# A hybrid decoder step in float32: norm factors made with tokens on partitions, and other work moved between engines in the convolution mixer

## The reference, cut to what matters

```python
def rms_norm(x, g):
    return x * rsqrt(mean(x * x, axis=-1) + 1e-6) * g

def conv_mixers(h, ...):                       # h: RMS-normed input, D = 1024
    z = h @ w_in                               # 1024 -> 2560 = 20 columns of 128
    glu = z[..., :512] * sigmoid(z[..., 512:1024])
    af = causal_dwconv31(glu) + bias
    an = (af - mean(af)) * rsqrt(var(af) + 1e-5) * lg + lb   # over 512 channels
    a_out = an * sigmoid(an)
    G, C, X = z[..., 1024:1536], z[..., 1536:2048], z[..., 2048:2560]
    b_out = G * causal_dwconv3(C * X)
    return concat(a_out, b_out) @ w_out        # residual add follows
```

## Time and profile before

| | |
|---|---|
| median of 3 runs | 2745.41 us (2745.17 to 2745.77) |
| the profiled execution | 2743.18 us |
| its span | 2741.4 us |
| mean granted clock of TensorE | 0.987 |
| busy: PE, PEld | 2634.0, 2465.1 us |
| busy: DVE, ACT, POOL | 1435.6, 627.5, 782.2 us |

### The profile page before, as it was taken

One profiled execution on the slowest core, in us unless ns is written; L12 is line 12 of the kernel. 1 busy time (PEld: TensorE's weight loads), 2 busy tenths in 40 slices (PEclk: granted clock), 3 DMA queues, 4 the chain that ended last, 5 costly groups with the idle time before them and its releaser, 6 DMA issues.

```text
span 2741.4 us, 41727 instructions
## 1 busy us (share of the span) xinstructions
PE 2634.0 (96%) x17498; PEld 2465.1 (90%) x17498; DVE 1435.6 (52%) x1985; ACT 627.5 (23%) x930; POOL 782.2 (29%) x432
## 2 busy tenths in 40 slices
PE   6999699999999999999999999979999999999996
PEld 6988699999999999997777777759999999999995
DVE  6899856444444444456555555561544444444445
ACT  4110133111111111133333333342311111111111
POOL 5323325332233333340011011023433333233332
PEclk9999899999999999999999999999999999999997
DMA  6433294444444444643443444423111111111111
GB/s 198 161 131 123 92 180 167 164 168 169 169 169 169 169 168 164 219 159 123 143 167 127 166 153 155 148 91 135 47 47 47 42 44 47 47 47 47 47 42 64
DMA packets 93863, 336.70 MB, mean 123 GB/s; under 512 B 22528, under 2 KB 39808, under 8 KB 91136
## 3 DMA queue, kind: packets, MB, share of 16 engines
q1 hardware_dynamic: 93696, 334.20, 36.6%
HBM read 315.88 MB, written 152.25 MB: 171 GB/s over the span
## 4 chain that ended last, share of the span: by engine, by line
PE 87%; DVE 9%; issue 1%; ACT 1%; POOL 1%; DMA 0%; POOLq 0%; DVEq 0%; SPq 0%; ACTq 0%
PE reg L620 44%; PE reg L656 19%; PE reg L847 9%; DVE g L1458 4%; PE reg L725 3%; PE reg L827 3%; PE ob L883 2%; PE reg L868 1%; PE reg L800 1%; DVE neg_s L1685 1%; PE ob L868 1%; PE reg L936 1%; PE reg L638 1%; PE reg L923 1%; PE ob L699 1%
## 5 line engine op out<-in xcount | busy, mean ns | idle before, releaser
L620 PE MATMUL reg<-xs,w_sp 128*128 128x352 f32 x8208 | 1347.1, 326 | 33.8 <-DVE xs L1424 20.8
L620 PEld LDWEIGHTS reg<-xs,w_sp 128*128 128x128 f32 x8208 | 1335.3, 189 | 41.7 <-issue 30.3
L382 POOL TENSOR_TENSOR w_sp<-w_raw,w_sp 128x1024 fp32r<-128x1024 f32 x172 | 426.5, 2480 | 1068.2 <-ACT w_sp L377 1066.5
L656 PE MATMUL reg<-hid,w_sp 128*128 128x352 f32 x3168 | 514.3, 324 | 0.0
L656 PEld LDWEIGHTS reg<-hid,w_sp 128*128 128x128 f32 x3168 | 511.5, 188 | 0.0
L377 ACT ACTIVATE w_sp<-w_raw 128x1024 fp32r<-128x1024 f32 x172 | 182.3, 1060 | 1138.4 <-PE reg L620 713.1
L1435 DVE TENSOR_TENSOR h<-reg,h 128x1056 f32<-128x1056 f32 x200 | 251.4, 1257 | 305.0 <-PE reg L656 235.0
L847 PE MATMUL reg<-xs,w_sp 128*128 128x352 f32 x1512 | 279.6, 332 | 0.0
L1591 DVE TENSOR_TENSOR g<-reg,rst 128x1056 f32<-128x1056 f32 x44 | 55.4, 1259 | 414.7 <-PE reg L620 414.7
L847 PEld LDWEIGHTS reg<-xs,w_sp 128*128 128x128 f32 x1512 | 240.6, 189 | 17.7 <-issue 17.6
L400 POOL TENSOR_TENSOR w_sp<-w_raw,w_sp 128x1024 fp32r<-128x1024 f32 x21 | 49.9, 2375 | 479.9 <-ACT w_sp L395 461.1
(11 more groups left out here) (178 smaller groups left out, 1978.5 us busy)
## 6 DMA issues: line engine op xcount, KB each, us to landing
w_raw<-in_wstream SPq DMA_DIRECT2D x193, 512.0 KB, 3.6
out_sk<-in_cache_k SPq DMA_DIRECT2D x16, 4088.0 KB, 15.4
out_sv<-in_cache_v SPq DMA_DIRECT2D x16, 4088.0 KB, 15.3
kvr<-in_kva SPq DMA_DIRECT2D x16, 2048.0 KB, 9.3
kvr<-in_kvb SPq DMA_DIRECT2D x16, 1536.0 KB, 6.9
wt<-in_wtab SPq DMA_DIRECT2D x16, 512.0 KB, 5.1
h<-in_xT SPq DMA_DIRECT2D x4, 1056.0 KB, 10.0
h_spill<-h SPq DMA_DIRECT2D x8, 528.0 KB, 2.6
```

What stands on the lines that cost most here:

```text
L382: nc.gpsimd.tensor_tensor(w_sp[:, u % 3, 1, :], w_raw[:, u % 3, :], w_sp[:, u % 3, 0, :].bitcast(F32), ALU.subtract).then_inc(w_lo, 1)
L620: mm = nc.tensor.matmul(out[:, t, :], w[:, wh, k * P:(k + 1) * P], xs[:, xh, k, t * TS:(t + 1) * TS], start=(n == 0 and wh + xh == 0), sto ...
L656: mm = nc.tensor.matmul(out[:, t, :], w[:, wh, kk * 512 + m * P:kk * 512 + (m + 1) * P], hid[:, par_g, kk, xh, t * TS:(t + 1) * TS], start ...
```

## The change

1. **Norm factors with tokens on partitions**, at three places (first norm, LayerNorm variance, last norm). `token_sums`: nine matmuls, each with 128 tokens of `acc` as the stationary operand and one column of the 1/1024 matrix, so that the sums lie on 128 partitions x 9 columns. Square root (`compact_std`) and reciprocal (`compact_recip`) work on these 9 columns (`cs`). Nine further matmuls (`spread_sample`, `spread_half`) multiply a column of `cs`, repeated 128 times, by the identity, which puts the factors back on every partition. ScalarE copies them out of PSUM; the LayerNorm's products read PSUM directly. The norms in front of layer 0's FFN, attention and layer 1's FFN stay as they were.
2. **First squares**: eight buffers instead of two, and the sums on VectorE (`first_square`), between its `gain_lo` steps. The very last add of the last norm is on VectorE too. `rst` squared (`rst2`) is made once on ScalarE and used at C, so that POOL's product there goes.
3. **Weight remainders of units 4 to 22** are made on VectorE (`mixer_lo`), between its taps.
4. **Taps**: 96 beside the units 1 to 16; the other ten behind the input units, beside the B projection. `MEAN_USE` moves from the first to the fifth B use, `VAR_USE` from the fifth to the seventh. The sample convolution works in two halves, since `prod` gets its own, smaller place.
5. **SP**: no cache copies before unit 45; then one at every fifth unit to 90 (10 pieces), and 22 pieces at every third unit from 122 on. The states are stored one by one between unit loads 31 to 40; the waits in front of the FFN state come after unit 28.

The core of the diff (places that only follow from these are left out):

```diff
-MEAN_USE, VAR_USE = B_USE[0], B_USE[4]
+MEAN_USE, VAR_USE = B_USE[4], B_USE[6]
...
+            for u in range(3, 29):
+                load_unit(sp, u, u % 3)
             sp.wait_ge(x_lo, 2 * KD)
             sp.wait_ge(x_hi, 2 * KD)
             load_ffn_state(0)
+            for u in range(29, 95):
+                load_unit(sp, u, u % 3)
+                if 31 <= u < 41:
+                    if u == 31:
+                        sp.wait_ge(ysum_ok, 1)
+                    dst, src = states[u - 31]
+                    sp.dma_start(dst, src).then_inc(st_out, 16)
+                elif u >= 45 and u % 5 == 0:
+                    copy_piece(*pieces.pop())
...
+            for u in range(121, NUNITS + 1):
+                load_unit(sp, u, u % 3)
+                if u % 3 == 2 and pieces:
+                    copy_piece(*pieces.pop())
...
+            def token_sums(src):
+                for j, lo in enumerate(BLOCKS):
+                    mm = nc.tensor.matmul(ob[:, 1, j:j + 1], src[:, lo:lo + P], ones[:, 0:1], start=True, stop=True)
+                return mm
+            def spread_half(x):
+                for j in range(4):
+                    mm = nc.tensor.matmul(ob[:, x, j * P:(j + 1) * P], cs[:, 4 * x + j:4 * x + j + 1].to_broadcast([P, P]),
+                                          ident[:, :], start=True, stop=True)
+                return mm
...
-            first_units(0, 2, 0, 0)
+            in_proj(0, FIRST[0], x_at=0)
+            pe.wait_ge(sum_ok, KD)
+            token_sums(acc).then_inc(tk_full, 1)
+            in_proj(1, FIRST[1], part=(0,))
+            pe.wait_ge(r_ok, 1)
+            spread_sample(ob[:, 0, 0:NS]).then_inc(st_full, 1)
+            spread_half(1).then_inc(half_full, 1)
+            pe.wait_ge(std_ok, 1)
+            spread_half(0).then_inc(st_full, 1)
+            in_proj(1, FIRST[1], part=range(1, KD))
...
-                        sample_sums()
+                        token_sums(acc).then_inc(tk_full, 1)
...
+                        if k == 0 and r == VAR_USE:
+                            pe.wait_ge(r_ok, 2)
+                            spread_sample(ob[:, 0, 0:NS]).then_inc(ln_full, 1)
+                            spread_half(1)
+                            pe.wait_ge(std_ok, 3)
+                            spread_half(0).then_inc(ln_full, 1)
...
-            column_means(NAMED["stats4"], (sum_ok, SQ0[4] + KD), acc)
+            pe.wait_ge(sum_ok, SQ0[4] + KD)
+            token_sums(acc).then_inc(tk_full, 1)
+            pe.wait_ge(r_ok, 3)
+            spread_sample(reg[1][:, 0, 0:NS])
+            spread_half(1).then_inc(half_full, 1)
+            spread_half(0).then_inc(st_full, 1)
...
-                square(0, m, h[:, m, :])
+                nc.scalar.activation(sq_first[m], h[:, m, :], ACT.Square).then_inc(sq_ok, 1)
...
-            std_parts(2)
+            act.wait_ge(std_ok, 2)
+            nc.scalar.activation(rst2[:, :], rst[:, :], ACT.Square).then_inc(r2_ok, 1)
...
-            for m in range(KD):
-                add_square(0, m)
...
-                elif kind == "C":
-                    pool.wait_ge(free, FIRST[u] + 1)
-                    nc.gpsimd.tensor_tensor(tmp[:, :], tmp[:, :], rst[:, :], ALU.mult).then_inc(cr_ok, 1)
...
+            def mixer_lo(u):
+                dve.wait_ge(w_hi, cnt(u))
+                nc.vector.tensor_tensor(w_sp[:, u % 3, 1, :], w_raw[:, u % 3, :], w_sp[:, u % 3, 0, :].bitcast(F32),
+                                        ALU.subtract).then_inc(w_lo, 1)
...
             for u, (kind, c) in enumerate(MIX_ORDER):
                 mixer_step(kind, c, FIRST[u])
-                if u >= 1:
-                    for tc, tk in TAPS[PER * (u - 1):PER * u]:
+                if 1 <= u < 17:
+                    for n, (tc, tk) in enumerate(TAPS[PER * (u - 1):PER * u]):
+                        if n == 2:
+                            mixer_lo(u + 3)
                         conv_tap(tc, tk)
+                elif u in (17, 18):
+                    mixer_lo(u + 3)
             for c in range(CA):
                 rest_lo(1, c, c, cb[:, c, :])
+            mixer_lo(22)
+            rest = TAPS[PER * 16:]
+            for n, (tc, tk) in enumerate(rest):
+                if n == 3:
+                    add_to_h(B_USE[0], 0)
+                if n == 7:
+                    add_to_h(B_USE[1], 1)
+                conv_tap(tc, tk)
+            add_to_h(B_USE[2], 2)
+            add_to_h(B_USE[3], 3)
...
-            for m in range(4):
-                add_to_h(B_USE[m], m)
...
+            add_to_h(B_USE[4], 4)
+            add_to_h(B_USE[5], 5)
+            compact_recip(2)
...
             for c in range(CA):
-                nc.vector.tensor_tensor(Y[c], Y[c], tmp[:, :], ALU.mult).then_inc(yn_ok, 1)
-            add_to_h(B_USE[5], 5)
+                y = Y[c][:, 0:NP_].rearrange("p (x t) -> p x t", x=2)
+                nc.vector.tensor_tensor(y, ob[:, :, :], y, ALU.mult).then_inc(yn_ok, 1)
+                nc.vector.tensor_tensor(Y[c][:, NP_:], Y[c][:, NP_:], tmp[:, NP_:], ALU.mult).then_inc(yn_ok, 1)
```

More of the change, by code:

```diff
@@ L63, in plan_uses @@
 def plan_uses():
-    first, last, named, n = {}, {}, {}, 0
+    first, last, n = {}, {}, 0
     def unit(u, k=1):
@@ L429, in build @@
         sqb = [sil[:, PAD:], tmp[:, :]]
+        sq_first = [cb[:, 0, :], cb[:, 1, :], cb[:, 2, :], cb[:, 3, :], spare[:, :], tmp[:, :], sil[:, PAD:], g1[:, PAD:]]
+        BLOCKS = [P * j for j in range(NP_ // P)] + [T - P]
+        NBLK = len(BLOCKS)
         block = ctx.enter_context(nc.Block())
@@ L1799, in _ @@
             ffn(1)
-            factor(NAMED["stats4"], rst[:, :], 10)
+            dve.wait_ge(sq_ok, SQ0[4] + KD)
+            dve.wait_ge(sum_ok, SQ0[4] + KD - 1)
+            nc.vector.tensor_tensor(acc[:, :], acc[:, :], sqb[(SQ0[4] + KD - 1) % 2], ALU.add).then_inc(sum_ok, 1)
+            compact_recip(3)
+            dve.wait_ge(std_ok, 11)
             for m in range(KD):
```

173 lines of the change are left out of this document (81 added, 92 removed).

## The result

| | before | after |
|---|---|---|
| median, same chip | 2745.29 us (4 runs) | 2721.14 us (2719.57 to 2722.13, 4 runs) |
| profiled execution | 2743.18 us | 2722.13 us |
| its span | 2741.4 us | 2720.3 us |
| granted clock of TensorE | 0.987 | 0.989 |

The ratio of the times is 0.9911, with a 95% interval of 0.9894 to 0.9929: 0.9% faster, clear of noise, by 24 us in the medians and 21.1 us in the two traced executions. The forecast was 2722 and 23.4 us off the traced execution.

The account below looks back on a forecast made before the run. TensorE, busy 2634.0 of 2741.4 us, was taken as the bound. Gains of 1.8 + 13.1 + 5.5 + 3.0 = 23.4 us off 2743.18 gave 2719.8, and 2722 from the median; range 2711 to 2734.

Parts of the forecast that it names:

- the input units: Mixer's input units: TensorE's stops go because VectorE keeps up; gain 13.1 us, bounds 7 to 13.1.
- The ten taps: Mixer: ten taps go behind the input units, taking 13 us of VectorE's work out of them.
- Start: First norm to the end of unit 1: ends at 51.3 instead of 53.1; gain 1.8 us, bounds 6.5 to -1.5.
- Output units: End of the input units to the first A matmul: 60.6 us instead of 69.1; gain 5.5 after clock, bounds 8.5 and 0.
- the 3.0 us for the clock: Output units: taken off the 8.5 us gain because both stops can lower the clock for the matmuls behind them.
- The rival "clock": Low clock at the start, variance and end costs 2.2 + 4.4 + 1 us more: 2729; chance 0.17.
- Between the FFN and the last matmul: FFN, attention and second FFN, to the last matmul: no change, 0 us.
- End: Last matmul to first output step: that step at 2725.1 instead of 2727.81; gain 3.0 us, 2.7 to 7.1.
- Copies: Cache copies, none in the mixer and 22 of 32 beside the last FFN: priced at nothing.
- VectorE as the bound: Rival 1, the 16 units with taps and remainders: VectorE becomes the bound, 2785 us, slower; chance 0.05.
- The late chain: Rival 3, output units: the LayerNorm chain in four uses of cover is later, 8 us more, 2730; chance 0.14.
- The end at the good bounds: Rival 4, everything at its good bound: start 6.5, no clock loss, end 7, about 2710 us; chance 0.12.

Follow-up runs that it names:

- the first experiment: Changed kernel with the weight remainders of units 4 to 22 back on GpSimd: 2733.36 us, ratio to before 0.9957.
- the experiment: Changed kernel with the old norm factors at the first norm alone, first squares staying on VectorE: 2716.97 us, ratio to before 0.9899.
- the last experiments: Changed kernel with old first-norm factors, a GpSimd split held back, LayerNorm chain off GpSimd and idle matmuls: 2704.74 us; without the first of these: 2710.99 us.
- the kernel with all four edits: Changed kernel with old first-norm factors, GpSimd's third split held back, LayerNorm chain off GpSimd, 22 idle matmuls before the last token sums: 2704.74 us.
- the one without the first-norm edit: Changed kernel with GpSimd's third split held back, LayerNorm chain off GpSimd and 22 idle matmuls, token factors kept at the first norm: 2710.99 us.

## Why the prediction was right, and where it was not

**Right as a whole**: 2721.1 against 2722, by a sum in which two terms came out high and two low. That the total fits to 1 us is partly luck: between the traced executions, for which the sum was made, the gain is 21.1 us and not 23.4, and errors of 0.6 to 2.4 us per stretch cancel in part. The largest term, the input units, was right in size (13.8 for 13.1) and in its main mechanism: GpSimd's remainders made the stops in these units, and undone they bring back 11.3 us of the stretch. The ten taps, 13 us in the forecast's sum for these units, were not needed there: put back, they leave the units at 240.5 us and cost 9.5 us in front of the output units. The last 2.5 us of the 13.8 are not traced to one part; the product at C that left GpSimd and VectorE's earlier start were not tried alone. The 104 taps cost 102.5 + 40.8 = 143 us, near the 147 that the forecast left them for 105. Each remainder frees 2.1 us of VectorE by the first experiment, 37.5 us for 18 of them, where the forecast took 36 us (three quarters of the taps' excess of 48) for the remainders and the product at C together. The units took 240.5 us where I had 241.5; by the forecast's own prices (18 x 11.8 and 3 x 9.9) it should have been 242.1, and the gain 12.5.

The Trainium skill's rule that the two engines exclude each other for a whole instruction ("SBUF — State Buffer", "Who interferes with whom") would have given 2.4 per remainder; the 2.1 measured is near it.

**Start, 1.8, measured 1.2.** The sums began at 34.5, as forecast (35.0). The small matmuls at full clock are 0.12 us as I took them (2.17 / 18 = 0.12). But the clock fell behind them (0.50 from 37.3 to 40.7), which cost the spreads and the 9 matmuls between them 1.7 us. And the step priced the moved squares and the new factors in one sum and never set the new factors against the old ones: 4.5 us of small matmuls against 2.3 of column sums. With the 1.7 us of the clock that is 3.9, and the experiment shows a loss of 3.7 us on TensorE's path, inside a gain of some 5 us made by moving the squares. One edit hid the other's price.

**Output units, 5.5, measured 3.1.** The schedule held within 2 us: stops of 3.63 and 3.76 us (3.4 and 3.8), the second on GpSimd's `w_sp` (the token sums begin at E+46.0, E being the end of the input units, forecast E+44.3; the mean sums stood at E+28.5, 1.5 later than forecast, behind the first stop's clock). The term that failed is the 3.0 us for the clock. The low stretch is 10.2 us long, and from the first sum to the matmul behind the spreads it is 9.75 us (348.44 - 338.69) where the full clock gives 5.41 (337.93 - 332.52, last fence above): 4.3 us, and 1.5 more behind the first stop (25.07 for 23.6). So 5.8 us stand where the forecast had 3.0, and 8.5 less 5.8 is 2.7, near the 3.1 measured. The rival "clock" thus had its mechanism and overstated its price: 2.2 more at the start (measured 1.7), 4.4 more around the variance (2.8), 1 more at the end (0.7 less). No run puts the LayerNorm's old factors back or moves the two uses alone, so how the 3.1 us divide between the token factors and the new order of the uses is open.

**Between the FFN and the last matmul, 0, measured -0.8.** This is inside the spread of the stretch, which varies by 5.2 us over the executions traced, so no effect of the change is shown.

**End, 3.0, measured 3.7.** First output step 13.2 us after the last matmul instead of 14.2; the forecast's own figures (2725.1 for 2727.81) give a gain of 2.7, and 3.0 was taken. Sums 4.00 (4.4) and spreads 4.2 (4.5) were a little cheaper, and the last add brought its 1.3. That the clock is low there and doubles the price was right.

**Copies, 0**: right, shown by the copies put back.

**Rivals.** VectorE as the bound did not come (no stop in the units). The late chain did not come either: VectorE ended the sum over channels (L1501) at 317.5, E+24.9 for the forecast's E+25.5, 3.7 us before TensorE read it, and the variance sums were 1.7 us late, nearly all of it the 1.5 us that TensorE's own clock cost before the mean. The end at the good bounds needed the clock, which only the edits of the last experiments gave back in part.

## What to carry to other kernels

Before a cheaper form replaces a dear one, ask which engine is the bound at that place: the same token-wise factors were worth 2.4 us at the end, where everything waits, and cost some 3.7 at the start, where the 6.6 us reciprocal ran beside TensorE's work. A stop of TensorE just ahead of small matmuls is paid twice, so take the last releaser out of the chain (here a weight remainder queued on GpSimd) before making the chain's steps cheaper. And where gains are a few us of 2700, compare the length of the stretch that was edited, not the totals.

## What the runs showed of the hardware

- One-column float32 matmuls cost 0.12 us per instruction at the full clock (2.10 to 2.17 us for 18) and 0.22 at half (4.00); 128-column ones 0.127 (2.03 for 16 where the clock stayed full) and up to 0.235 (3.76). In such a row the number of columns hardly matters, so putting tokens on partitions saves VectorE's columns, not TensorE's instructions.
- The clock can fall in such a row of small matmuls without a stop before it: in the kernel with the LayerNorm chain off GpSimd it was at half for about 3.4 us, mostly in the spreads, with TensorE busy since 296.98; in the kernel with all four edits the spreads were slow too (3.51 us), while in the one without the first-norm edit the same spreads ran at full clock (2.03). So it was in the first norm: the same 16 spreads took 2.03 us in four of the nine executions with the same work up to there, and 2.52 to 3.37 in the other five.
- A VectorE step of 1.25 us with two SBUF inputs took 3.45 beside one 3.12 us GpSimd step, and GpSimd's own step grew from 2.35 to 3.12 us: both lose. Short steps with one SBUF input lost as well: with the remainders on GpSimd the copy of 32 columns (L1543) took 1.24 us in the mean, for 0.18 without.
